# Filler products on TensorE inside the blocked recurrence of a two-layer model

## What is computed

```python
def wkv_scan(state0, r, w, k, v, kk, a, reverse):
    ...
    xs = (tm(r), tm(w), tm(k), tm(v), tm(-kk), tm(kk * a))

    def step(S, inp):
        r_t, w_t, k_t, v_t, nkk_t, b_t = inp
        sa = jnp.einsum('bhvk,bhk->bhv', S, nkk_t)
        S = S * w_t[:, :, None, :] + sa[..., None] * b_t[:, :, None, :] + v_t[..., None] * k_t[:, :, None, :]
        return S, jnp.einsum('bhvk,bhk->bhv', S, r_t)

    S_final, ys = lax.scan(step, state0, xs, reverse=reverse)
...
for d in range(2):
    ...
    Sc, yc_d = wkv_scan(S0, rc, wdc, kdc, vrc, kkc, adc, rev)
    _, y_d = wkv_scan(Sc, r, wd, kd, vr, kk, ad, rev)
    y_lat = y_lat + y_d
```

## Time and profile before

| | |
|---|---|
| median of 3 runs | 4721.98 us (4721.06 to 4729.0) |
| the profiled execution | 4731.52 us, of which the span from the first to the last instruction is 4729.9 us |
| mean granted clock of PE | 0.84 of full speed |
| PE busy | 4021.9 us (85% of the span) |
| DVE, ACT busy | 2436.4 us (52%), 1672.5 us (35%) |
| recurrence, 2860 to 3820 us | PE busy 717.18 of 960 us, granted clock 0.60 |

### The profile page before, as it was taken

One profiled execution on the slowest core, in us unless ns is written; L12 is line 12 of the kernel. 1 busy time (PEld: TensorE's weight loads), 2 busy tenths in 40 slices (PEclk: granted clock), 3 DMA queues, 4 the chain that ended last, 5 costly groups with the idle time before them and its releaser, 6 DMA issues.

```text
span 4729.9 us, 86122 instructions
## 1 busy us (share of the span) xinstructions
PE 4021.9 (85%) x33052; PEld 3565.8 (75%) x33052; DVE 2436.4 (52%) x4265; ACT 1672.5 (35%) x2326; POOL 23.3 (0%) x46
## 2 busy tenths in 40 slices
PE   7999777677989999996999557777777788999998
PEld 6999332456989999995889345555556688999998
DVE  3744776444647777445335334554554445444443
ACT  3545333212445555333123231222222134555433
POOL 0000000000000000000000000000000000000000
PEclk9999667567999999998999676665666589999999
DMA  4555667122545555552224000000000044555553
GB/s 156 185 184 191 218 224 273 36 71 91 176 142 179 185 178 185 173 181 99 90 97 150 0 7 3 4 4 4 4 4 4 2 144 143 184 180 184 177 180 122
DMA packets 80531, 569.33 MB, mean 120 GB/s; under 512 B 9472, under 2 KB 9728, under 8 KB 15456
## 3 DMA queue, kind: packets, MB, share of 16 engines
q1 hardware_dynamic: 78048, 558.50, 34.0%
q0 software_dynamic: 2304, 8.36, 0.5%
HBM read 564.73 MB, written 2.10 MB: 120 GB/s over the span
## 4 chain that ended last, share of the span: by engine, by line
PE 78%; DVE 12%; issue 5%; ACT 3%; DMA 2%; DVEq 1%; ACTq 0%; POOL 0%; SPq 0%; POOLq 0%
PE po L256 16%; PE po L258 16%; PE po L257 16%; PE po L1158 5%; PE pa L822 4%; PE po L822 2%; PE po L443 1%; PE pa L302 1%; PE po L1241 1%; DMA s_ct<-s_c 1%; PE pa L1705 1%; DVE hf L313 1%; DMA ada_buf<-ada 1%; DVE k_nrm L1641 1%; PE po L1249 1%
## 5 line engine op out<-in xcount | busy, mean ns | idle before, releaser
L244 DVE TENSOR_TENSOR w_lo<-raw,w_hi 128x1024 fp32r<-128x1024 f32 x880 | 1039.3, 1202 | 606.8 <-ACT w_hi L237 588.8
L256 PE MATMUL po<-hh,w_lo 128*128 128x256 f32 x4256 | 1207.5, 284 | 24.3 <-DVE hh L337 12.6
L257 PE MATMUL po<-hh,w_hi 128*128 128x256 f32 x4256 | 1207.0, 284 | 0.0
L258 PE MATMUL po<-hh,w_hi 128*128 128x256 f32 x4256 | 1207.0, 284 | 0.0
L237 ACT ACTIVATE w_hi<-raw 128x1024 fp32r<-128x1024 f32 (+1 forms) x877 | 898.4, 1038 | 802.1 <-PE po L258 620.2
L256 PEld LDWEIGHTS po<-hh,w_lo 128*128 128x128 f32 x4256 | 819.4, 193 | 25.6 <-issue 25.5
L257 PEld LDWEIGHTS po<-hh,w_hi 128*128 128x128 f32 x4256 | 819.4, 193 | 0.0
L258 PEld LDWEIGHTS po<-hh,w_hi 128*128 128x128 f32 x4256 | 819.3, 193 | 0.0
L256 PE MATMUL po<-f_hi,w_lo 128*128 128x256 f32 x1408 | 400.5, 284 | 6.1 <-DVE f_lo L1338 6.1
L258 PE MATMUL po<-f_hi,w_hi 128*128 128x256 f32 x1408 | 400.1, 284 | 0.0
L257 PE MATMUL po<-f_lo,w_hi 128*128 128x256 f32 x1408 | 400.1, 284 | 0.0
(11 more groups left out here) (539 smaller groups left out, 6703.4 us busy)
## 6 DMA issues: line engine op xcount, KB each, us to landing
raw<-ffn_up SPq DMA_DIRECT2D x176, 1024.0 KB, 4.9
raw<-w_in SPq DMA_DIRECT2D x112, 1024.0 KB, 4.9
raw<-ffn_down SPq DMA_DIRECT2D x64, 1024.0 KB, 4.9
raw<-ada SPq DMA_DIRECT2D x56, 1024.0 KB, 5.1
ada_buf<-ada SPq DMA_DIRECT2D x40, 1024.0 KB, 6.7
raw<-w_out SPq DMA_DIRECT2D x32, 1024.0 KB, 4.9
raw<-ffn_down SPq DMA_DIRECT2D x32, 768.0 KB, 4.2
raw<-glu SPq DMA_DIRECT2D x16, 1024.0 KB, 5.0
```

Source lines behind the costliest of these rows:

```text
L244: dve.tensor_tensor(w_lo[:, k % 4, 0:width], raw[:, k // 2, (k % 2) * PW:(k % 2) * PW + width], w_hi[:, k % 4, 0:width].bitcast(F32), ALU. ...
L256: pe.matmul(po[bank][:, 0:T], lo, act_hi[:, t, :], start=first and n == 0, stop=False)
L257: pe.matmul(po[bank][:, 0:T], hi, act_lo[:, t, :], start=False, stop=False)
L258: mm = pe.matmul(po[bank][:, 0:T], hi, act_hi[:, t, :], start=False, stop=end)
```

## The change

A fifth stream W is added on PE alone. Each of its turns issues one product of the 128x128 `k_bd` with 256 columns of `k_masks` into the bank `I[3]`, which nothing reads at that time; it waits for nothing and signals nothing. The order of all other turns stays: without its 16 W the new `PERIOD` is the old one. The 15 halves with an inversion get 16 fillers each, 240 in all (the last l half gets none).

```diff
-        PERIOD = "V C V C C V C V C C V C V C C V C V C P C V P O V P O V P O P O P O P P P".split()
+        PERIOD = "V C V W C W C W V W C W V W C W C W V W C W V W C W C W V W C W V W C P C V P O V P O V P O P O P O P P P".split()
...
-        def phases(eng, prep, inverse, chunk, post):
+        def phases(eng, prep, inverse, chunk, post, filler=None):
...
             with eng.Fori(0, 7) as j:
-                woven(C=chunk(eng, j, "c"), V=inverse(eng, j, "l"), P=prep(eng, j + 1, "c"))
-                woven(C=chunk(eng, j, "l"), V=inverse(eng, j + 1, "c"), P=prep(eng, j + 1, "l"), O=post(eng, j))
-            woven(C=chunk(eng, 7, "c"), V=inverse(eng, 7, "l"))
+                woven(C=chunk(eng, j, "c"), V=inverse(eng, j, "l"), P=prep(eng, j + 1, "c"), W=filler)
+                woven(C=chunk(eng, j, "l"), V=inverse(eng, j + 1, "c"), P=prep(eng, j + 1, "l"), O=post(eng, j), W=filler)
+            woven(C=chunk(eng, 7, "c"), V=inverse(eng, 7, "l"), W=filler)
             woven(C=chunk(eng, 7, "l"), O=post(eng, 7))
...
+        def filler_pe(pe):
+
+            while True:
+                pe.matmul(I[3][:, 0:T], k_bd[:], k_masks[:, 0:4, :], start=True, stop=True)
+                yield
...
         def rk_pe(pe):
-            phases(pe, prep_pe, inverse_pe, chunk_pe, post_pe)
+            phases(pe, prep_pe, inverse_pe, chunk_pe, post_pe, filler_pe(pe))
```

## The result

The changed kernel takes 4806.32 us in the median of four runs (4802.24 to 4811.68), against 4721.52 us before in the same session: a ratio of 1.0179, 95% interval 1.0161 to 1.0197, or 85 us. The forecast was 4795 us.

What follows compares the result with a forecast made beforehand. PE's own stream bounds low-clock sections. Fillers add 63 us in eight c and 10 us in seven l sections: +73 on the profiled 4731.5 gives 4805, less its 9.5 us above the median, 4795 us; range 4765 to 4835.

Steps and rivals of the forecast that it cites:

- Bound by PE's own stream: Sections at low clock: PE's own work sets their length, added work lengthens them almost in full; what follows is shifted.
- Price of a filler: In each section: 1.15 us per filler low, 0.60 high; 16 add 18.1 us low, 8.4 high after waits and overlap.
- the waits: Fillers cover PE's 0.3 us wait for ACT ahead of L1705 and, at high clock, 0.22 us for DVE.
- the overlap: L1695 starts 0.24 us before the last inversion product ends; a filler between costs 0.20 us low, 0.16 high.
- What the clock is worth: High clock shortens work by factor 0.67 in c, 0.60 in l sections without fillers; all high 17.2 and 20.9 us.
- the eighth: Eighth c section, which no L1443 closes, counted like the other seven at +7.9 us.
- When it rises: Clock taken to rise 9.7 us into c and 15 us into l sections, adding 63 and 10 us in all.
- The rule weighed: Skill says array activity releases the clock, so fillers raise it early; its 0.43 us price lowers the sum about 35.
- Early rise: Rival, chance 0.25: clock rises 5 us into c, 7 us into l sections; +33 us, 4755 us.
- Faster: Rival, chance 0.10: clock high after the first inversion product, 2.4 us in, with 0.51 us fillers; -10 us, 4712 us.

## Why the prediction was right

**Bound by PE's own stream.** Right. The sections grew by what PE had to do more, and what follows them moved with them unchanged.

**Price of a filler.** The row-to-row distances were taken as 1.15 and 0.60 us and are 1.15 and 0.63. With the waits and the overlap counted, 16 fillers were put at 18.1 us low and 8.4 us high in either section. They are 53.48 - 34.98 = 18.5 us (l, low), 8.9 us (l, high) and 7.8 us (c, high). A c section that stays low with whole fillers was not seen. An estimate from the one that rose latest (20.9 us low, 33.69 us in all, against 25.04 us all high) is 42.7 us where the prediction had 43.6.

**What the clock is worth.** Right for c: 17.2 us all high. Off for l: 20.9 us forecast from a single stretch of 3.42 us, 22.3 us measured. That is 1.4 us for an all-high section without fillers and 1.9 us with them (31.2 against 29.3), the rest being the price of a filler. With the measured 31.2 us all high and 53.5 us all low an l section comes to 15 + 38.5 x 0.583 = 37.4 us instead of 36.0, and the mean measured is 37.6. This is the mis-sized term of the sum. It made the l sections +10 us where they are +21. The c sections were put at +63 and are +54 for seven, and the eighth, taken like the others at +8, lies in a rest of the span that grew by 3.5 us in all. So the two errors partly cancel, and the 2.4 us ahead of the first section take off some more (73 us forecast, 76 in the spans, 85 in the medians).

**When it rises.** The averages, 10.7 and 15.5 us, are near the 9.7 and 15 that I chose. No row gave the 15, so that it came near is luck in good part. The picture behind the two was wrong. I had the c sections rise at one time, as four of seven do before, and they scatter over 16 us, and the l sections over 18. A mean was right where each single value was not, and the run with fillers in l halves alone shows how little fixed it is: no rise before the last microsecond of an l section in its profiled execution. Had I forecast that kernel by the same steps, 4732 us would have been the answer and 4820 the result.

**The rule weighed.** By the row, PE busy in the profile did not release the clock. The runs go further: fillers on a quarter or half of the array, in the same places and for as long or nearly so, never released it, and whole ones did. The Trainium skill's statement ("TensorE: Matmul & The Clock Gate", section "What's actually happening") that activity of the array releases the clock agrees with the whole fillers, and with the partial ones only if activity means more than an instruction under way. Its price by columns and passes, 0.43 us, is what fillers behind each other take: six at the high level took 2.86 us, of which the last is 0.70, so they start 0.43 us apart. Between products of other shapes, where the change puts them, it was too low: 0.63 measured.

**The rivals.** Early rise (4755) did not come. Faster (4712) needed a high clock from the first filler and a filler of 0.55 us or less. The run with six ahead and the sixteen inside grants the first half of it in full, and with 0.63 us a filler the result is 1.0007: no change, which is where the condition put it.

What stays open is why the same instructions reach 2.4 GHz after 3.5 us in one half and after 21 in another, and why three sections in the run with fillers in l halves alone never do. No run here controls the moment at which a section begins, so none can tell.

## What to carry to other kernels

A filler product belongs into a wait of TensorE, ahead of the stretch that is to run fast, and not among products that already keep the engine busy: six in a wait of 5 to 8 us took 105 us off, sixteen in a busy section added 85. Price it at both clock levels from rows in which a product stands between others of another tile shape, and price the clock from a whole section at the high level. Then look at the wait that is left behind the last filler, since fillers that run at the high level are over sooner, and profile every section: the number and place that held the clock here were found by trying.

## What was not expected of the hardware

- Whole-array products of 256 fp32 columns among quarter-array products let the clock rise in all 14 sections; the same products on half or a quarter of the array let it rise in none. That is no rule: the whole ones in l halves alone raised it in no l section of the profiled execution before its last microsecond.
- A high clock, once granted, held through sections of 17 to 31 us in which PE was busy only 85 to 96% of the time, while sections that were busy 94% (before) and 98% (52.05 us with half fillers) at 1.2 GHz stayed there.
- A wait of 1.29 us ahead of an l section kept the level, waits of 2.43 and 2.77 us were followed by its loss 0.5 and 1.5 us later. That is no rule either: the eighth c section of the kernel with fillers behind both kinds of sections kept the level behind a wait of 2.50 us, and two l sections with ten fillers ahead lost it 3.9 us in without a wait.
